# Branch A's sums of squares: fp32r products of a high and a low part, and squares added on VectorE ahead of the ones products

## What is computed

```python
h = _rmsnorm(x, g_pre); u = h @ w_in          # a_cq (512), a_ckv (256), a_kr (64), a_z (1024), ...
qa  = (_rmsnorm(a_cq, a_g_cq) @ a_w_uq).reshape(b, s, A_HEADS, A_NOPE + A_ROPE)      # 128 + 64
kva = (_rmsnorm(a_ckv, a_g_ckv) @ a_w_ukv).reshape(b, s, A_HEADS, A_NOPE + A_V)      # 128 + 128
qn = _rmsnorm(qa[..., :A_NOPE], a_g_q[:A_NOPE])
qr = _rope(_rmsnorm(qa[..., A_NOPE:], a_g_q[A_NOPE:]), *rope_a)
kn = _rmsnorm(kva[..., :A_NOPE], a_g_k[:A_NOPE])
kr = _rope(_rmsnorm(a_kr, a_g_k[A_NOPE:]), *rope_a)
o_a = _mla_attention(qn, qr, kn, kr, kva[..., A_NOPE:])
```

## Time and profile before

| | us |
|---|---|
| median of 3 runs | 3167.55 (3167.39 to 3168.92) |
| the profiled execution's own time | 3167.51 |
| its span, first to last instruction | 3165.9 |
| PE busy | 3144.4 (99%) |
| DVE busy | 2111.4 (67%) |
| ACT busy | 1737.0 (55%) |
| share of the 16 DMA engines used by the queue of loads | 58.7% |

### The profile page before, as it was taken

The page is one execution under the profiler, slowest core; times in us unless marked ns, Lnnn a source line. Parts: engine busy times, 40 slices in busy tenths (PEclk is TensorE's granted clock), DMA queues, the critical chain, the costliest instruction groups (busy, mean ns, idle before and its releaser), DMA issues.

```text
span 3165.9 us, 52112 instructions
## 1 busy us (share of the span) xinstructions
PE 3144.4 (99%) x18246; PEld 2745.6 (87%) x18246; DVE 2111.4 (67%) x2717; ACT 1737.0 (55%) x2285; POOL 0.2 (0%) x4
## 2 busy tenths in 40 slices
PE   8999999999999999999999999999999999999999
PEld 7888888888888788888888888888888888888888
DVE  7677575666667676666666555777666666655575
ACT  5685444444445556656565555645665555555563
POOL 0000000000000000000000000000000000000000
PEclk9999999999999999999999999999999999999999
DMA  7656655555556565565556655666556555666555
GB/s 228 193 169 199 198 186 167 185 176 172 174 172 210 169 179 151 155 197 173 176 169 191 190 181 175 187 198 182 155 156 193 177 173 172 191 184 183 178 183 175
DMA packets 569809, 571.67 MB, mean 181 GB/s; under 512 B 26352, under 2 KB 565488, under 8 KB 569712
## 3 DMA queue, kind: packets, MB, share of 16 engines
q1 hardware_dynamic: 569712, 570.42, 58.7%
HBM read 568.25 MB, written 2.10 MB: 180 GB/s over the span
## 4 chain that ended last, share of the span: by engine, by line
PE 98%; DVE 1%; ACT 1%; issue 0%; DMA 0%; SPq 0%; DVEq 0%; ACTq 0%
PE pg L531 91%; PE pa L767 1%; PE pa L784 1%; PE pa L774 1%; PE pa L743 1%; PE pa L785 1%; PE pa L531 0%; PE pa L698 0%; PE pa L734 0%; DVE hl L1274 0%; ACT hl L932 0%; DMA raw<-w_in 0%; PE pa L874 0%; DVE uT L1355 0%; DVE xres L1721 0%
## 5 line engine op out<-in xcount | busy, mean ns | idle before, releaser
L531 PE MATMUL pg<-hT,hl 128*128 128x512 f32 x11456 | 2035.9, 337 | 0.7 <-DVE hl L1274 0.5
L531 PEld LDWEIGHTS pg<-hT,hl 128*128 128x128 f32 x11456 | 1751.9, 188 | 263.6 <-issue 6.9
L1274 DVE TENSOR_TENSOR hl<-raw,hl 128x1024 fp32r<-128x1024 f32 (+1 forms) x1071 | 1254.3, 1208 | 337.8 <-ACT hl L932 332.1
L932 ACT ACTIVATE hl<-raw 128x1024 fp32r<-128x1024 f32 (+1 forms) x1071 | 1084.2, 1043 | 309.8 <-PE pg L531 294.9
L531 PE MATMUL pg<-uT,hl 128*128 128x256 f32 (+1 forms) x3712 | 639.3, 333 | 17.1 <-DVE hl L1479 7.2
L531 PEld LDWEIGHTS pg<-uT,hl 128*128 128x128 f32 x3712 | 558.3, 190 | 93.8 <-issue 14.7
L940 ACT ACTIVATE corr<-pg 128x512 f32<-128x512 f32 x286 | 170.0, 594 | 845.7 <-PE pg L531 845.5
L531 PE MATMUL pg<-hl,hT 128*128 128x256 f32 (+1 forms) x1792 | 317.9, 336 | 0.0
L1281 DVE TENSOR_TENSOR work<-pg,corr 128x512 f32<-128x512 f32 (+1 forms) x154 | 105.8, 687 | 308.2 <-ACT corr L940 308.1
L531 PEld LDWEIGHTS pg<-hl,hT 128*128 128x128 f32 x1792 | 274.9, 188 | 40.7
L1281 DVE TENSOR_TENSOR gat<-pg,corr 128x512 f32 (+1 forms) x71 | 48.9, 689 | 149.4 <-ACT corr L940 149.4
(11 more groups left out here) (182 smaller groups left out, 1362.0 us busy)
## 6 DMA issues: line engine op xcount, KB each, us to landing
raw<-w_in SPq DMA_DIRECT2D x791, 512.0 KB, 4.7
raw<-w_br SPq DMA_DIRECT2D x96, 512.0 KB, 4.5
raw<-w_out SPq DMA_DIRECT2D x64, 512.0 KB, 4.7
raw<-w_rnn SPq DMA_DIRECT2D x32, 512.0 KB, 4.8
raw<-w_o SPq DMA_DIRECT2D x32, 512.0 KB, 5.3
raw<-w_att SPq DMA_DIRECT2D x16, 512.0 KB, 4.1
raw<-w_uq SPq DMA_DIRECT2D x16, 384.0 KB, 3.6
tab<-tabs SPq DMA_DIRECT2D x5, 896.0 KB, 7.3
```

The lines of the kernel that those rows point to most:

```text
L531: return nc.tensor.matmul(out, lhsT, rhs, start=start, stop=stop, skip_group_check=True)
L932: nc.scalar.activation(hl4[:, j % 2, 0, a:a + n], raw[:, bass.ds(j % 2 * UC + a, n)], ACT.Copy)\
L1274: tt(hl4[:, j % 2, 1, a:a + n], raw[:, bass.ds(j % 2 * UC + a, n)], hl4[:, j % 2, 0, a:a + n].bitcast(F32), ALU.subtract).then_inc(lo_done, 1)
```

## The change

Branch A's squares are handled as those of B and C are. ACT's one event q becomes q0 (after u0: the two q tiles and the rope part, 768 wide) and q1 (after u1: the two k tiles, 512 wide), each a Square, a wait for it, and a Copy of the high part to fp32r. DVE subtracts: for q0 after its own u0, for q1 after the copies of keys and values; the latter raises `sq_ready`. The rope part moves from place 4 of `qk_l` to place 2, the keys to 3 and 4. PE's norm has two fp32r matmuls of 256 columns and four of 512. In the head, DVE adds the squares of a_cq and of a_ckv up at c = 4, and PE has three fp32 matmuls instead of seven. The new tiles `sq_a` lie in memory that `mix` has too.

```diff
 ACT_EVENTS
-    "A": events("u0-1 q u2 h6 norm h7-8 s0-1 h9-10 t0-1 h11 p0-1"),
+    "A": events("u0 q0 u1 q1 u2 h6 norm h7-8 s0-1 h9-10 t0-1 h11 p0-1"),
 DVE_EVENTS
-    "A": events("u0-2 h6 norm rot h7-8 s0-1 x0-1 h9-11 p0-1 lo0-1"),
+    "A": events("u0 q0 u1-2 h6 norm rot h7-8 s0-1 x0-1 h9-11 p0-1 lo0-1"),
...
+        with nc.sbuf_tensor("mix_r", [P, 10 * S], F32R) as mix_r:
+            sq_a = [mix_r[:, 5 * S * h:5 * S * h + 5 * S].rearrange("p (t n) -> p t n", n=S) for h in range(2)]
+        squares_a = [slice(0, 3), slice(3, 5)]
...
             def squares_sum(kind, l):
...
-                nc.tensor.matmul(pa3[:, 2, 0:S], blk, nt3[:, 4, :], start=True, stop=True)
+                pe.wait_ge(ones_ready, l + 1)
+                if kind == "A":
+                    for h in range(2):
+                        mm(pa3[:, 2, 0:S], sums_of_r["B"], sq_a[h][:, 2, :], h == 0, h == 1)
                 for b in range(2):
-                    ins = nc.tensor.matmul(pa3[:, b, :], ones, nt3[:, 2 * b:2 * b + 2, :].rearrange("p t n -> p (t n)"),
-                                           start=True, stop=True)
+                    for h in range(2):
+                        part = sq_a[h][:, 3 * b:3 * b + 2, :].rearrange("p t n -> p (t n)") if kind == "A" else \
+                            u3[:, 8 + 2 * h + b, :]
+                        ins = mm(pa3[:, b, :], sums_of_r["B" if kind == "B" else "C"], part, h == 0, h == 1)
                 ins.then_inc(norm_done, 1)
...
                     if c == 6:
-                        pe.wait_ge(a_sq, l + 1)
-                        for t in range(4):
-                            nc.tensor.matmul(pa3[:, 0, 0:S], ones, m3[:, 6 + t, :], start=t == 0, stop=t == 3)
-                        for t in range(2):
-                            nc.tensor.matmul(pa3[:, 0, S:], ones, m3[:, 10 + t, :], start=t == 0, stop=t == 1,
-                                             skip_group_check=True)
+                        pe.wait_ge(a_summed, l + 1)
+                        nc.tensor.matmul(pa3[:, 0, 0:S], ones, m3[:, 6, :], start=True, stop=True)
+                        nc.tensor.matmul(pa3[:, 0, S:], ones, m3[:, 10, :], start=True, stop=True, skip_group_check=True)
...
                     elif what == "q":
-                        act.wait_ge(evac_done, c + 4)
+                        act.wait_ge(evac_done, c + 3 + j)
                         act.wait_ge(u_ready, 2 * pi)
-                        nc.scalar.activation(nt3[:, 0:5, :], qk_l[:, 0:5, :], ACT.Square).then_inc(sq_ready, 1)
+                        t = squares_a[j]
+                        steps.done(nc.scalar.activation(nt3[:, t, :], qk_l[:, t, :], ACT.Square))
+                        nc.scalar.activation(sq_a[0][:, t, :], nt3[:, t, :], ACT.Copy).then_inc(a_sq_hi, 1)
...
+            def squares_lo(n, j):
+                t = squares_a[j]
+                dve.wait_ge(a_sq_hi, 2 * n + j + 1)
+                return tt(sq_a[1][:, t, :], nt3[:, t, :], sq_a[0][:, t, :].bitcast(F32), ALU.subtract)
...
                             nc.vector.tensor_copy(v_l, both[1]).then_inc(evac_done, 1)
+                            squares_lo(4 * l + p, 1).then_inc(sq_ready, 1)
...
+                    elif what == "q":
+                        squares_lo(4 * l + p, j)
...
                     elif c == 4:
                         lambda_value(l)
+                        dve.wait_ge(a_sq, l + 1)
+                        tt(m3[:, 10, :], m3[:, 10, :], m3[:, 11, :], ALU.add)
+                        steps.done(tt(m3[:, 6:8, :], m3[:, 6:8, :], m3[:, 8:10, :], ALU.add))
+                        tt(m3[:, 6, :], m3[:, 6, :], m3[:, 7, :], ALU.add).then_inc(a_summed, 1)
```

More of the change, by code:

```diff
@@ L290, in build @@
             sem(n) for n in ("a_sq", "a_sum", "a_rs", "a_val", "a_hi", "a_ready", "a_rot", "kr_ready"))
-        a_part, rope_r, roped = sem("a_part"), sem("rope_r"), sem("roped")
+        a_sq_hi = sem("a_sq_hi")
+        a_part, rope_r, roped, a_summed = sem("a_part"), sem("rope_r"), sem("roped"), sem("a_summed")
         kr_landed = [[sem(f"kr_landed{j}{h}") for h in range(2)] for j in range(2)]
@@ L719, in rotate @@
             def rotate():
-                nc.tensor.matmul(pa3[:, 2, 0:S], tab[:, T_R:T_R + P], qk_l[:, 4, :], start=True, stop=True)\
+                nc.tensor.matmul(pa3[:, 2, 0:S], tab[:, T_R:T_R + P], qk_l[:, 2, :], start=True, stop=True)\
                     .then_inc(rot_done, 1)
             def squares_sum(kind, l):
[L725 to L731, removed]
-                nc.tensor.matmul(pa3[:, 2, 0:S], blk, nt3[:, 4, :], start=True, stop=True)
+                pe.wait_ge(ones_ready, l + 1)
+                if kind == "A":
+                    for h in range(2):
+                        mm(pa3[:, 2, 0:S], sums_of_r["B"], sq_a[h][:, 2, :], h == 0, h == 1)
                 for b in range(2):
-                    ins = nc.tensor.matmul(pa3[:, b, :], ones, nt3[:, 2 * b:2 * b + 2, :].rearrange("p t n -> p (t n)"),
-                                           start=True, stop=True)
+                    for h in range(2):
+                        part = sq_a[h][:, 3 * b:3 * b + 2, :].rearrange("p t n -> p (t n)") if kind == "A" else \
+                            u3[:, 8 + 2 * h + b, :]
+                        ins = mm(pa3[:, b, :], sums_of_r["B" if kind == "B" else "C"], part, h == 0, h == 1)
                 ins.then_inc(norm_done, 1)
@@ L747, in scores_with_rope @@
                     for tq in (1, 0):
-                        piece(e, tq, qk_l[:, e, :], qk_l[:, 2 + e, :], tq == 1, False)
+                        piece(e, tq, qk_l[:, e, :], qk_l[:, 3 + e, :], tq == 1, False)
                 pe.wait_ge(kr_ready, l + 1)
@@ L753, in scores_with_rope @@
                     for tq in (1, 0):
-                        ins = piece(e, tq, qk_l[h, 4, :], kr[h, :], False, tq == 0)
+                        ins = piece(e, tq, qk_l[h, 2, :], kr[h, :], False, tq == 0)
                     ins.then_inc(scores_done, 1)
@@ L1606, in pair @@
                             nc.vector.tensor_copy(qk_l[:, 0:2, :], both[0])
-                            nc.vector.tensor_copy(qk_l[:, 4:5, :], both[1][:, 0:1, :]).then_inc(evac_done, 1)
+                            nc.vector.tensor_copy(qk_l[:, 2:3, :], both[1][:, 0:1, :]).then_inc(evac_done, 1)
                         elif n == 2:
@@ L1610, in pair @@
                             dve.wait_ge(a_part, 4 * l + p + 1)
-                            nc.vector.tensor_copy(qk_l[:, 2:4, :], both[0]).then_inc(evac_done, 1)
+                            nc.vector.tensor_copy(qk_l[:, 3:5, :], both[0]).then_inc(evac_done, 1)
                             dve.wait_ge(half_done, 2 * (u + 2) + 2)
                             nc.vector.tensor_copy(v_l, both[1]).then_inc(evac_done, 1)
+                            squares_lo(4 * l + p, 1).then_inc(sq_ready, 1)
                         elif n in (3, 5) and 1 in halves:
@@ L1635, in pair @@
                             dve.wait_ge(rope_r, 4 * l + p + 1)
-                            stt(qk_l[:, 4, :], qk_l[:, 4, :], v2[:, W_AQR:W_AQR + 1], nt3[:, 9, :], ALU.mult, ALU.mult)\
+                            stt(qk_l[:, 2, :], qk_l[:, 2, :], v2[:, W_AQR:W_AQR + 1], nt3[:, 9, :], ALU.mult, ALU.mult)\
                                 .then_inc(normed, 1)
@@ L1639, in pair @@
                         stt(qk_l[:, 0:2, :], qk_l[:, 0:2, :], v2[:, gq:gq + 1], nt3[:, 5:7, :], ALU.mult, ALU.mult)
-                        ins = stt(qk_l[:, 2:4, :], qk_l[:, 2:4, :], v2[:, gk:gk + 1], nt3[:, 7:9, :], ALU.mult, ALU.mult)
+                        keys = qk_l[:, 3:5, :] if kind == "A" else qk_l[:, 2:4, :]
+                        ins = stt(keys, keys, v2[:, gk:gk + 1], nt3[:, 7:9, :], ALU.mult, ALU.mult)
                         if kind == "B":
@@ L1651, in pair @@
                             dve.wait_ge(rot_done, 4 * l + p + 1)
-                            rotate(qk_l[:, 4:5, :], pa3[:, 2:3, 0:S], nt3[:, 9:10, :], 1, roped)
+                            rotate(qk_l[:, 2:3, :], pa3[:, 2:3, 0:S], nt3[:, 9:10, :], 1, roped)
                         else:
@@ L1833, in _ @@
                     tt(sq_new[:, 0, :], sq_sum[:, 0, :], sq_sum[:, 1, :], ALU.add).then_inc(n_sum, 1)
-ACT_PAIR_STEPS = {"A": 2, "B": 4, "C": 2}
+ACT_PAIR_STEPS = {"A": 4, "B": 4, "C": 2}
 def tables():
```

## The result

The changed kernel takes 3175.8 us (median of 12 runs, 3174.86 to 3176.71), the kernel before on the same chips 3167.55 (12 runs, 3166.52 to 3168.92). The ratio is 1.0026, with a 95% interval of 1.0018 to 1.0034: slower, by 8.25 us. The forecast was 3175.7.

The account below looks back on a forecast made before the run. TensorE's weight matmuls were taken to bound the kernel. Eight pairs losing 1.46 us each (11.7) less 3.5 gained in the heads gave +8.2 on 3167.51, so 3175.7 us, range 3167 to 3181.

Parts of the forecast that it names:

- Bound: Whole kernel: nine tenths of the chain is TensorE's weight matmuls; time saved there counts, and any wait before PE is lost in full.
- Saved on PE: PE's sums: per pair, fp32r matmuls of 1.16 us replace fp32 ones of 2.16, saving 1.00, 8.0 in all; heads save 3.46.
- The head: Start of each layer: eight fewer PE records save 1.73 us, 3.46 in all; DVE's additions, at most 1.6, hide in idle time.
- before h6: PE's wait for the first half of DVE's `lo`, late because q0 delays `hi` of unit 3: 0.36 us a pair.
- before the norm: PE's wait for the keys' Square, Copy and DVE subtraction, behind the delayed copy of the keys: 1.90 us a pair.
- before rot: PE's wait for DVE's L1636, which follows ACT's `hi` and moves by 1.65 us: 0.20 us a pair.
- filling: Extra time of PE's first matmul behind a wait, 0.51 us against 0.39 in a stream: 0.12 us.
- Nothing new after rot: Rest of the pair: keys ready about 1.1 us ahead of the scores, loads as far ahead as before, nothing carried over.
- the rival of later steps: Scores and softmax chain: another half us a pair lost there, or by extra register work in loops, 3179.7 us; chance 0.08.
- the rival of the clock: PE's idling in the pairs drops the clock to 1.2 GHz for one half unit each: 22 us more, 3198; chance 0.03.
- The second: No measurable change: the pairs' delay is half covered, a pair loses 0.4 to 1.2 us, 3167 to 3173 us; chance 0.20.
- The first: Faster: the pairs' new ACT and DVE work goes into idle time, 3156.1 us, or 3161.1 if q0 alone does; chance 0.11.

Follow-up runs that it names:

- e7_all: Changed kernel with q0 behind `hi` of unit 3, PE waiting separately for the squares' parts, and the rope part's scaling ahead of unit 5's first half: 3157.36 us.
- e1_head: Kernel before with the head's edit alone (VectorE adds the squares, three fp32 matmuls instead of seven): 3165.22 us.
- e8_actonly: Kernel before with only ScalarE's q0 (Square and Copy, 768 wide) added ahead of the high part of unit 3, the Copy unused: 3179.27 us.
- e2_pairs: Changed kernel with the head's edit taken back, so only branch A's pairs are changed: 3179.15 us.
- e3_q0late: Changed kernel with q0 moved behind `hi` of unit 3 and its subtraction behind the copy of the values, same instructions: 3163.64 us.
- e4_keys32: Changed kernel with the keys' squares as before (one Square of 512, one fp32 matmul, no Copy or subtraction), q0 left in place: 3170.59 us.
- e6_split: e3_q0late with TensorE waiting for the two parts of the squares one after the other, by a semaphore of its own: 3163.53 us.

## Why the prediction was right

**Bound.** TensorE's list bounds the kernel and every wait in front of it counts: PE's busy time fell and the time rose.

**Saved on PE.** In a stream the six fp32r matmuls take 1206.63 - 1205.46 = 1.17 us (`e7_all`), by the forecast 1.16; behind a wait, 1.26 (1208.55 - 1207.29). The three fp32 matmuls that went had taken 2.16, and `e7_all` keeps 1.02 a pair where 1.00 was worked out. The head: 1.73 a layer by the trace, 2.8 us in all by `e1_head` where 3.46 was forecast, within what that run can tell. VectorE's additions took 1.40 us, not 1.6 at most, and all of it out of idle time.

**q0.** It took 1.64 us, against 1.63 by width from branch B's rows. The 768 wide instruction takes 0.85, so the fixed part is 0.2 us, as the forecast read it from its rows. The forecast also had 1.87 us for q0, an estimate with the 0.3 us an ACTIVATE of the Trainium skill ("ScalarE: Activation LUTs", rules for kernel authors). The page gives that figure for a bias that is a [128,1] pointer operand; q0's Square and Copy are given none, so the figure is not for them, and the 0.2 us measured here is no disagreement with the page.

**The three stalls.** All three are where they were forecast, and in the same order of size (us, first pair):

| | forecast | measured, by starts |
|---|---|---|
| before h6 | 0.36 | 1202.69 - 1202.45 = 0.24 |
| before the norm | 1.90 | 1207.29 - (1202.69 + 2.79) = 1.81 |
| before rot | 0.20 | 1211.53 - (1208.55 + 2.79) = 0.19 |
| rot later by | 1.46 | 17.53 - 16.19 = 1.34 |
| a pair longer by | 1.46 | 1.39 |

(1202.45 is u1's start and the 8.45 us from u1 to h6 of before, 1202.94 - 1194.49. The stalls are 2.24 together, and behind a wait the sums save 2.16 - 1.26 = 0.90, which gives rot's 1.34. In layer 2 the wait before rot is 0.09 instead of 0.19, and a pair is 1.33 longer.)

The forecast has rot 0.12 us too late, and the rows tell where that comes from. It let ACT's keys Square follow the copy of the keys by 0.12 us, as before. It follows by 0.03 (the copy ends at 1205.19, the Square starts at 1205.22), in all 8 pairs here and in every run that has q0; in the kernel before and in `e1_head` it is 0.12 in all 8. No run tells why. So ACT's list behind it, `hi` of unit 4 first, moves by 1.55 instead of 1.65 (1206.42 - 1194.00 against 1205.36 - 1194.49), and DVE's scaling with it. That is 0.09 of the 0.12. The other 0.03 is the step from DVE's end to PE's start, which the forecast put at 0.17 and which is 0.14 at rot.

That 0.17 was 0.05 for the semaphore and 0.12 of filling, added to the start of PE's first matmul behind a wait. At h6 and the norm the step is 0.05 to 0.06, so there the filling does not move the start. It makes the distance to the next one longer (1.26 for 1.17 over the norm's six), and where another wait follows it is swallowed there; behind rot none follows, and there it adds 0.05 to the pair. In `e8_actonly` the norm is 12.54 - 11.24 = 1.30 later than before (1208.07 - 1195.53, and 1205.73 - 1194.49) where 1.53 was expected: 0.12 of that is the filling, and 0.09 again the Square's earlier start. The filling then comes back behind the norm's wait, 0.09 us, so most of the 0.16 that the expectation had too much is the Square's earlier start.

**How much of the match is luck.** The total came out within 0.1 us of the forecast, but not its parts. The pairs were put at 11.7 and cost 11.1 by `e2_pairs`, some 10.9 by the rows; the heads were put at 3.5 and gave 2.8 by `e1_head`, 3.5 by the rows. By the rows alone the change comes to 7.4 us, so some 0.8 of the 8.25 stand neither in the pairs nor in the heads. The mechanism is right; the last microsecond is not explained.

**Nothing new after rot.** No wait of PE's appeared at the scores, the transposes or the next pair, so the rival of later steps did not come. Nor did the rival of the clock: the granted clock in the pair stayed 1.00, its 2.4 GHz level, though PE stood idle before h6, the norm and rot. The Trainium skill ("TensorE: Matmul & The Clock Gate", Part 1) says that idling is what lowers the clock; in the pairs of both layers the granted clock is 1.00 in every run, so none shows such a fall. This is the row of that stretch (us; busy PE, PEld, DVE, ACT, POOL; clock; DMA):

```profile
1189.50:1227.40 37.90, 36.25 (x227) 32.12 (x226) 27.58 (x44) 25.48 (x38) 0.00 (x0) 1.00 0.50 150
```

**The other rivals.** The second, a pair losing 0.4 to 1.2 us, fell with the 1.33 to 1.39 measured. The first, that the work goes into idle time, named the point where it would be decided: rot, with 0.19 us of slack. `e3_q0late` and `e7_all` show that it was a matter of place: the 3156.1 us that it would have given is, within 1.3 us, what `e7_all` takes. The Trainium skill ("Perfetto Trace Analysis", on optimizing Scalar/DVE operations) says that where Scalar and Vector aren't saturated but cause bubbles on other engines, breaking up instructions may let work complete sooner. `e4_keys32` shows both sides of that: behind the copy of the keys its Square of 512 takes 0.63 us where the one of 1280 took 1.28, but the piece split off stands in front of `hi` of unit 3, and the pair got longer.

What stays open: the time up to the first pair varies from run to run by a few us. In the profiled run of `e6_split` the first u1 starts at 1191.40, in that of `e3_q0late` at 1194.60, at equal medians (3163.53 and 3163.64). Nothing was tried on that, and the comparisons by pair do not depend on it. Nor is it known why the Square follows the copy 0.09 us sooner than before.

## What to carry to other kernels

Where one engine is the bound and the others are half idle, look at where an engine's idle time stands in its own list before putting work on it. ScalarE was idle 2.85 us in each pair, but behind the instruction that the bound engine needed next, and 1.64 us put in front of that instruction cost 1.4 a pair (`e8_actonly`). Work out the slack of each wait on the way, since the one with the least decides, and two of them side by side hide one another: against `e3_q0late`, taking either away gained 0.1 or 2.4 us, both together 6.3. And take an operation's cost from the same operation at another width elsewhere in the kernel; q0's was right to 0.01 us. The step from one engine to the next is less certain: taken from the same place in the kernel before, it was off by 0.09.

## What the runs showed of the hardware

- A wait before a matmul shows in two places besides the idle time: its own record is longer (0.70 us instead of 0.60 for the first two records of the norm in `e8_actonly`), and the next one starts later by 0.1 us.
- The profile's idle time for PE is less than what is lost, since the records' ends are modelled and reach past the next start: the norm's wait is given as 1.54 us, by the starts it is 1.81.
- The same handover, from DVE's copy of the keys to ACT's Square, took 0.12 us in one program and 0.03 in another, each time in all 8 pairs.
